# A weight load issued one step later, and the shift row multiplied six tiles earlier, in the first MLP of a two-block fp32 kernel

## What is computed

```python
def _squared_relu_mlp(h, w1, w2):
    a = jax.nn.relu(h @ w1)
    return (a * a) @ w2
...
    x = x + _squared_relu_mlp(_rmsnorm(x, norm_mlp[layer]), mlp_w1[layer], mlp_w2[layer])
    return _rmsnorm(x, norm_final)
...
def ada_mod(cond, w, b):
    m = jax.nn.silu(cond) @ w + b
    return jnp.split(m, N_MOD, axis=-1)
...
        hx2 = modulate(rms_norm(x, norm2_g[l]), sh2, sc2)
        x = x + g2 * sqrelu_mlp(hx2, w_mlp1[l], w_mlp2[l])
```

## Time and profile before

| | |
|---|---|
| median of 3 runs | 2747.8 us |
| lowest, highest | 2745.17, 2748.24 us |
| the profiled execution: its time, its span | 2747.8 us, 2746.0 us |
| TensorE busy | 2674.3 us, 97% of the span |
| DVE, ACT busy | 1582.8 us (58%), 1074.9 us (39%) |
| the stage of the change | about 906 to 1257 us |

### The profile page before, as it was taken

The page is one execution under the profiler, slowest core; times in us unless marked ns, Lnnn a source line. Parts: engine busy times, 40 slices in busy tenths (PEclk is TensorE's granted clock), DMA queues, the critical chain, the costliest instruction groups (busy, mean ns, idle before and its releaser), DMA issues.

```text
span 2746.0 us, 41687 instructions
## 1 busy us (share of the span) xinstructions
PE 2674.3 (97%) x17264; PEld 2236.6 (81%) x17264; DVE 1582.8 (58%) x2224; ACT 1074.9 (39%) x1735; POOL 178.9 (7%) x153
## 2 busy tenths in 40 slices
PE   8999999999999999997899999999899999999999
PEld 7887878778888888886889878877787888888887
DVE  6445454476665797866525555566657656654443
ACT  6444454544434322126232443344445555521110
POOL 2222212300000000005100000000000000000000
PEclk9999999999999999999899999999999999999999
DMA  4111111213333786752323221121631333442221
GB/s 134 40 40 32 40 32 33 93 31 119 107 112 116 279 318 222 276 192 77 118 78 122 64 73 48 50 73 48 221 123 37 117 115 101 149 157 94 99 77 69
DMA packets 243676, 297.05 MB, mean 108 GB/s; under 512 B 10528, under 2 KB 190240, under 8 KB 243488
## 3 DMA queue, kind: packets, MB, share of 16 engines
q1 hardware_dynamic: 243488, 294.38, 32.0%
HBM read 238.77 MB, written 55.57 MB: 107 GB/s over the span
## 4 chain that ended last, share of the span: by engine, by line
PE 73%; ACT 4%; DVE 3%; DMA 1%; issue 1%; POOL 0%; SPq 0%; ACTq 0%; DVEq 0%
PE ps L841 8%; PE ps L850 8%; PE ps L844 8%; PE ps L807 7%; PE ps L809 7%; PE ps L811 7%; PE ps L529 2%; PE ps L513 2%; PE ps L1028 2%; PE ps L516 2%; PE ps L1029 2%; PE ps L1033 2%; PE ps L599 2%; PE ps L595 2%; PE ps L597 2%; PE ps L1003 1%
## 5 line engine op out<-in xcount | busy, mean ns | idle before, releaser
L1333 ACT ACTIVATE Whi<-Wraw 128x1024 fp32r<-128x1024 f32 x164 | 171.7, 1056 | 708.0 <-PE ps L850 433.3
L1882 DVE TENSOR_TENSOR Wlo<-Wraw,Whi 128x1024 fp32r<-128x1024 f32 x152 | 189.5, 1253 | 427.3 <-ACT Whi L1333 427.1
L807 PE MATMUL ps<-Bh,Ah 128*128 128x512 f32 x896 | 350.5, 391 | 5.3 <-ACT wb L1511 3.5
L809 PE MATMUL ps<-Bh,Al 128*128 128x512 f32 x896 | 349.2, 390 | 0.0
L841 PE MATMUL ps<-a_h,Whi 128*128 128x512 f32 x1024 | 316.0, 390 | 0.7 <-DVE R L1919 0.7
L844 PE MATMUL ps<-a_h,Wlo 128*128 128x512 f32 x1024 | 315.3, 389 | 0.0
L850 PE MATMUL ps<-a_l,Whi 128*128 128x512 f32 x1024 | 252.9, 389 | 0.0
L811 PE MATMUL ps<-Bl,Ah 128*128 128x512 f32 x640 | 249.0, 389 | 0.0
L595 PE MATMUL ps<-Whi,Hh 128*128 128x256 f32 x768 | 223.5, 291 | 7.6 <-ACT Hh L1364 7.6
L599 PE MATMUL ps<-Whi,Hl 128*128 128x256 f32 x768 | 220.0, 286 | 8.0 <-DVE Hl L1912 8.0
L841 PEld LDWEIGHTS ps<-a_h,Whi 128*128 128x128 f32 x1024 | 192.2, 188 | 41.4 <-DVE R L1919 1.1
(11 more groups left out here) (346 smaller groups left out, 4950.6 us busy)
## 6 DMA issues: line engine op xcount, KB each, us to landing
pair<-in_m_w SPq DMA_DIRECT2D x64, 512.0 KB, 5.4
a_scratch<-ub SPq DMA_DIRECT2D x128, 256.0 KB, 2.0
Wraw<-in_m_w SPq DMA_DIRECT2D x64, 512.0 KB, 4.2
a_r<-a_scratch SPq DMA_DIRECT2D x64, 512.0 KB, 5.3
Wraw<-in_w_in SPq DMA_DIRECT2D x56, 512.0 KB, 4.1
n<-in_w_ada SPq DMA_DIRECT2D x32, 512.0 KB, 5.0
mraw<-in_w_ada SPq DMA_DIRECT2D x32, 512.0 KB, 5.7
R<-in_xT SPq DMA_DIRECT2D x16, 512.0 KB, 4.5
```

The source lines that it names most:

```text
L807: e.matmul(o, h[:, k, :], Bh[x][:, k, :], start=first and k == 0, stop=False, skip_group_check=not first)
L809: e.matmul(o, l[:, k, :], Bh[x][:, k, :], start=False, stop=False, skip_group_check=not first)
L1333: e.activation(Whi[n % 4][:], Wraw[n % 2][:], ACT.Copy).then_inc(*S("w_hi").tick(n))
L1882: e.tensor_tensor(Wlo[n % 4][:], Wraw[n % 2][:], Whi[n % 4][:].bitcast(F), ALU.subtract).then_inc(*S("w_lo", "v").tick(n))
```

## The change

On SP, `feed` before an even tile no longer asks for one weight beyond `upto`. On TensorE the shift row is multiplied after tile (3, 2) in place of (4, 0), and ACT copies it in (3, 4) in place of (4, 2).

```diff
@@ tensor_program, mlp
-                            if j == 0 and c == 4 and m == 0:
+                            if j == 0 and c == 3 and m == 2:
                                 b, occ = take("shift_row")
                                 empty(b, occ)
                                 pe.wait_ge(S("shift_diag").at(0), S("const").at(0))
@@ sync_program
             for i in range(8):
                 for m in range(8):
                     if m % 2 == 0:
-                        feed(upto((0, "s2", i, m // 2)) + 1)
+                        feed(upto((0, "s2", i, m // 2)))
                     if i < 7:
                         for _ in range(1 + (m < 7)):
                             modulation()
@@ scalar_program
-                        if (i, m) == (4, 2):
+                        if (i, m) == (3, 4):
                             act.wait_ge(full_at("shift_row"))
                             e.activation(shr[:], tile("shift_row")[:], ACT.Copy).then_inc(*freed("shift_row"))
```

## The result

| | before | after |
|---|---|---|
| median of 4 runs each, same job | 2748.0 us | 2808.9 us |
| lowest, highest | 2745.2, 2748.6 us | 2806.4, 2809.8 us |
| ratio, 95% interval | | 1.0223, 1.0205 to 1.0240 |
| the profiled execution: its time, its span | 2747.8, 2746.0 us | 2810.8, 2809.0 us |

The change makes the kernel 60.9 us slower, 2.2%. The forecast was 2798 us, range 2774 to 2818.

The account below looks back on a forecast made before the run. TensorE, busy 97%, bounds the kernel; after the change a latency loop through SP, DMA, ACT and DVE does. 2747.8 + 48.5 (lateness at (7,1)) + 2 (clock) = 2798 us, range 2774 to 2818.

Parts of the forecast that it names:

- The loads: First MLP's second half: each weight load issues only after DVE's previous tile; 13.8 us a weight against TensorE's 10.88.
- E: Moment when DVE has finished an odd tile, its modulation steps included; SP issues the next weight 1.0 us later.
- landing: Time from a weight load's issue to its arrival, taken as 7.0, 7.4 or 5.8 us by stretch.
- The load lands in time: Rival: weight 5 lands in 3.3 us, no stall, 2748 us; or one stall, 2751; 5 in 100 together.
- the ring: Loop of SP issue, landing, ACT cast, DVE split, add and modulation steps, back to SP: 13.8 us a weight.
- The shift row: After (3,2) TensorE waits 10 us for DVE's diagonal; (3,3) starts 36 us late, 27 without the move.
- The relief: At (3,0) to (3,2) six empty modulation steps let SP issue two weights early; DVE catches up with TensorE.
- Second stretch: From (3,5) to (7,1): TensorE's four-tile lead is eaten by about (5,3); (7,1) ends up 48.5 us late.
- The clock: TensorE's lower clock costs 2 us, between 0 and 3.4, only behind the 10 us idle; elsewhere waits absorb it.
- Rival 3: Rival listed with the experiments: the lower TensorE clock makes the loss; no chance given there.
- Nothing later gives it back: From (7,1) on, modulation steps are used up and TensorE's 48.5 us lateness stays to the end.
- first stretch: Weights from (0,3) to (2,7): four weights take 52.7 us against 43.5, and (0,7) starts 2.6 us late.

Follow-up runs that it names:

- e3_one_tile_earlier: The changed kernel, but SP loads each weight one tile earlier, before the odd tile's two modulation loads instead of after them: 2745.9 us, ratio 0.9996.
- e4_weight_before_a: The changed kernel, but SP issues each weight load ahead of the a_r load instead of behind it: 2779.6 us, ratio 1.0103.
- e9_half_step: The changed kernel, but each DVE modulation step works on 512 of 1024 columns, leaving out half of each sum; loads stay whole: 2783.0 us, ratio 1.0119.
- e2_shift_only: The kernel before with only the two shift row edits, weights loaded as before: 2747.5 us, ratio 1.000.
- e7_second_half: The changed kernel, but for i under 3 weights are loaded as early as in the kernel before: 2770.1 us, ratio 1.0080.
- e6_first_half: The changed kernel, but from i = 3 on weights are loaded as early as in the kernel before: 2787.7 us, ratio 1.0141.

## Why the prediction was right, and where it was short

**The loads: right.** E, the issue, the landing, the cast and DVE follow each other as written; (0, 7) is 2.5 us late against 2.6 forecast. A pass of four weights took 53.5 and 54.0 us against 52.7. By the shift row 2.1 us more had gathered than forecast, 1.6 of them in the landings: the eight of these two passes add up to 55.0 us against 53.4. "The load lands in time" would need 4.1 us; the shortest landing of the ring in the profile after is 5.6. `e3_one_tile_earlier`, `e4_weight_before_a` and `e9_half_step` each change one member of the ring and the time follows.

**The shift row: right in its mechanism.** The wait was 10.5 us, forecast 10; the shift row started at 1091.3 - 1.0 = 1090.3, forecast 1088.2; `e2_shift_only` shows that without the late load it is free. Its share, 9 us, is 8 in place, but 1 to 4 in the time; the difference is open, as said.

**The relief: right.** From (3, 5) to (5, 0) nothing is lost further, and the lead is eaten between (5, 1) and (5, 3), as forecast.

**Second stretch: mis-sized.** From (3, 5) to (7, 1) 17.0 us were lost, forecast 12.2 (48.5 less 36.3). From DVE's add of (3, 5) to that of (6, 5) it was 161.9 us, forecast 157.1. The twelve landings in it add up to 85.3 us against 80.1 that the forecast's 5.8, 7.0 and 7.4 give (1.3 less where one modulation load fewer stands ahead). The term "landing" is where the sum was short: 5.2 us, about as much as the stretch was longer. The profile before could have told. In the same order, the two loads issued at 946.6 and 956.0 landed so,

```profile
DMA to landing us min/median/max: 7.4/8.2/9.0
```

and those at 1100.7, 1111.6 and 1122.5 took 7.6, 6.7 and 8.6; the earlier trace rows holds none of the five, and the forecast took 7.0 for this stretch's first loads. The 5.7 to 5.8 "where no a_r stands ahead" is also misread in one of its three loads: the one at 1175.64 has an `a_r` and a single modulation load ahead.

**The clock: right.** From the start of the shift row to that of (3, 5) it took 15.1 us (1091.30 to 1106.38), where the forecast has 12.8 at full clock: 2.3 us, forecast 2. In the ring the granted clock was 0.95 on average over 144 us, that is 1.2 instead of 2.4 GHz for about a tenth of it, 7 us of work. By this reading it cost nothing there, since DVE set the pace: TensorE still had to wait for its adds (14 times in the stage, 29.6 us), and from 936 to 1080 us none of DVE's waits was for TensorE. The Trainium skill (TensorE: Matmul & The Clock Gate, "A second HAM failure mode") says that frequent short idles between groups of matmuls make the clock swing; the trace agrees, with 0.95 after a steady 1.00 before. Rival 3 thus holds for some 5 of 61 us: these 2.3 and the 2.6 of the next point.

**"Nothing later gives it back": this step failed, in the other direction.** Later more was lost: 7.7 us at the end of the stage. When the ring opens at (7, 0), DVE is still behind by its whole queue. Its timeline after, the adds of (6, 7) and (7, 0):

```profile
1284.18 1.22 DVE L1919 TENSOR_TENSOR R<-ps,R 128x1024 f32<-128x1024 f32 x1
1285.74 1.22 DVE L1919 TENSOR_TENSOR R<-ps,R 128x1024 f32<-128x1024 f32 x1
```

TensorE had ended (7, 0) before it began (7, 1) at 1277.5, over 8 us earlier; in the kernel before the add of (7, 0) began at 1219.1, 0.3 us after (7, 1). From (7, 0) on each finished block is squared on ACT and summed on POOL, and TensorE multiplies the sums with ones between the last tiles (lines 612 and 615). Behind the late adds it waited 5.1 us for POOL and lost 2.6 us more, most of it at the lower clock (granted 0.61 from 1310 to 1316 us). The forecast counted TensorE's lateness at (7, 1) and left out DVE's own arrears, which matter as soon as somebody other than TensorE needs DVE. The wait is there in `e7_second_half` and every kernel whose second stretch is slow, and not in `e6_first_half`. `e4_weight_before_a` sets it apart from TensorE's own lateness: there nothing is lost from (4, 2) to (7, 0), and the 5.1 us are waited all the same. That the late adds reach POOL through ACT's squares is read from the traces; no run changed that path alone.

**The sum.** 2798.3 + 2.1 (first stretch) + 0.3 (clock) + 4.8 (second stretch) + 7.7 (end of the stage) + 1.0 (ahead of the stage) - 3.3 (after it) = 2810.9; the profiled execution took 2810.8. The mechanism and the sign were right; the total was 11 us short of the median, over half of it the end of the stage.

## What to carry to other kernels

A load in an in-order issue queue has no cover of its own: its cover begins when the queue's last wait ahead of it is released, so count from that release, and see who releases it. If the releaser is an engine that itself needs the load a step later, the loop costs its whole length each pass, whatever the busy shares say, and every member of it (an issue ahead, a landing, half a vector instruction) is then paid in full; one tile of earlier issue made all of it vanish. When lateness is reckoned for one engine, reckon also the arrears of the one it waits for: they fall due where a third engine needs its results.

## What was not expected of the hardware

- Behind two modulation loads of 512 KB and a load of `a_r`, the landing of one and the same 512 KB load swung from 6.0 to 8.1 us within the stage of the changed kernel, and up to 9.0 in the kernel before; with one modulation load fewer ahead it was 5.6 to 7.2. Three loads of one order are too few to take a landing from.
- Behind two modulation loads alone it was 5.7 and 5.8 us before, 5.9 and 6.2 in the profile after, 6.4 and 6.8 in `e4_weight_before_a`. An `a_r` issued 0.4 us behind the weight changed nothing that these landings show.
- The Trainium skill (DMA: Bandwidth & Descriptors, "Anatomy of one DMA") has 2.0 us plus the bytes over 436 GB/s, measured on DMAs that GpSimd issues; that makes an estimate of 3.2 us for 512 KB. SP's load that ran alone took 3.3, near that; the median of 6.9 that the ring paid is over twice as much.
- After the 10.5 us idle TensorE came back at 1.2 GHz, half of its 2.4 (granted 0.50 from 1091.3 to 1094.2 us): its four matmuls of the shift row lasted 3.75 us against 1.88. The waits of up to 3.6 us before had already brought the mean to 0.95.
